# Two of eight channel groups of a depthwise convolution computed by GpSimd, as a product and an addition per tap

## The reference

```python
def conformer_conv(glu_in, pw1_b, dw_w, dw_b, ln_g, ln_b, w_o, b_o):
    a, gate = jnp.split(glu_in + pw1_b, 2, axis=-1)
    h = a * jax.nn.sigmoid(gate)
    h = causal_dwconv(h, dw_w) + dw_b
    h = jax.nn.silu(layernorm(h, ln_g, ln_b))
    return h @ w_o + b_o
...
        y_a = gated_deltanet(qkv, z, beta_logit, a_logit, ...)
        y_b = conformer_conv(glu_in, ...)
        g_a, g_b = jnp.split(jax.nn.sigmoid(gates), 2, axis=-1)
        y = (g_a * y_a + g_b * y_b) @ mix_w_out[i]
```

## Time and profile before

| | us |
|---|---|
| median of 3 runs | 3380.99 (3378.2 to 3381.55) |
| span of the profiled execution | 3380.1 |
| the page shows outside the span | nothing |
| TensorE, VectorE, ScalarE, GpSimd busy | 3065.2, 2050.7, 1397.9, 74.2 |

### The profile page before, as it was taken

How to read it: one execution, slowest core, us unless ns; L and a number is a source line. 1 busy time by engine, 2 the same in 40 slices (tenths; PEclk the granted TensorE clock), 3 DMA queues, 4 the chain that set the end, 5 groups by cost and what they waited for, 6 DMA issues and landing times.

```text
span 3380.1 us, 48537 instructions
## 1 busy us (share of the span) xinstructions
PE 3065.2 (91%) x18678; PEld 2694.5 (80%) x18678; DVE 2050.7 (61%) x3081; ACT 1397.9 (41%) x2230; POOL 74.2 (2%) x98
## 2 busy tenths in 40 slices
PE   8999888899999998888998889976999999987998
PEld 8989766789898986677997568864897989774897
DVE  5559887555555798856555455552656665553555
ACT  4446422343433552333434334442444345442444
POOL 0000000000000000000000000000000000000000
PEclk9999999899999999988998779986999999886999
DMA  6555211255455441114553235540554555421453
GB/s 215 186 163 170 86 50 51 99 166 187 164 181 175 163 156 38 57 49 158 186 187 119 71 109 187 181 141 6 184 187 163 175 182 184 162 94 50 153 187 137
DMA packets 127386, 469.89 MB, mean 139 GB/s; under 512 B 14318, under 2 KB 14494, under 8 KB 125904
## 3 DMA queue, kind: packets, MB, share of 16 engines
q1 hardware_dynamic: 124128, 452.62, 40.0%
q0 software_dynamic: 3056, 14.39, 1.2%
HBM read 465.91 MB, written 1.05 MB: 138 GB/s over the span
## 4 chain that ended last, share of the span: by engine, by line
PE 82%; DVE 10%; ACT 4%; issue 2%; POOL 1%; DMA 0%; SPq 0%; DVEq 0%; ACTq 0%
PE ps L469 81%; DVE hc L1623 1%; DVE w_lo_part L1422 1%; ACT w_hi_part L1034 1%; PE ps L537 1%; ACT gdn_w L1248 1%; POOL stats L2044 1%; DVE x_res L1546 1%; ACT h_hi_part L1050 0%; DVE x_res L1558 0%; DVE xn L1552 0%; DVE x_res L1525 0%; DVE h_lo_part L1438 0%; DVE lke L1865 0%; DMA w_raw<-in_weights 0%
## 5 line engine op out<-in xcount | busy, mean ns | idle before, releaser
L1422 DVE TENSOR_TENSOR w_lo_part<-w_raw,w_hi_part 128x1024 fp32r<-128x1024 f32 x856 | 1028.8, 1218 | 684.7 <-ACT w_hi_part L1034 684.2
L1034 ACT ACTIVATE w_hi_part<-w_raw 128x1024 fp32r<-128x1024 f32 x856 | 884.4, 1055 | 621.2 <-PE ps L469 615.5
L469 PE MATMUL ps<-h_hi_part,w_hi_part 128*128 128x256 f32 x3424 | 987.1, 288 | 16.5 <-DVE h_lo_part L1440 11.6
L469 PE MATMUL ps<-h_lo_part,w_hi_part 128*128 128x256 f32 x3424 | 983.3, 287 | 0.0
L469 PE MATMUL ps<-h_hi_part,w_lo_part 128*128 128x256 f32 x3424 | 982.7, 287 | 0.0
L469 PEld LDWEIGHTS ps<-h_hi_part,w_hi_part 128*128 128x128 f32 x3424 | 673.3, 197 | 24.3 <-issue 17.4
L469 PEld LDWEIGHTS ps<-h_lo_part,w_hi_part 128*128 128x128 f32 x3424 | 672.9, 197 | 0.6
L469 PEld LDWEIGHTS ps<-h_hi_part,w_lo_part 128*128 128x128 f32 x3424 | 672.2, 196 | 0.0
L469 PE MATMUL ps<-w_hi_part,h_hi_part 128*128 128x512 f32 (+2 forms) x812 | 329.8, 406 | 12.3 <-DVE h_lo_part L1438 7.0
L469 PE MATMUL ps<-w_hi_part,hid_lo_part 128*128 128x512 f32 x864 | 340.9, 395 | 0.0
L469 PE MATMUL ps<-w_lo_part,hid_hi_part 128*128 128x512 f32 x864 | 340.9, 395 | 0.0
(11 more groups left out here) (307 smaller groups left out, 2590.2 us busy)
## 6 DMA issues: line engine op xcount, KB each, us to landing
w_raw<-in_weights SPq DMA_DIRECT2D x856, 512.0 KB, 3.4
row<-in_rows POOLq DMA_DIRECT2D x8, 1024.0 KB, 4.9
row<-in_rows POOLq DMA_DIRECT2D x8, 512.0 KB, 4.4
const<-in_const SPq DMA_DIRECT2D x1, 1152.0 KB, 13.8
x_res<-in_x SPq DMA_DIRECT2D x1, 1024.0 KB, 5.3
ple_p<-in_p POOLq DMA_DIRECT2D x4, 256.0 KB, 4.9
out<-x_res SPq DMA_DIRECT2D x2, 512.0 KB, 2.6
cols<-in_cols SPq DMA_DIRECT2D x1, 422.0 KB, 7.1
```

The costliest lines, as they stand in the source:

```text
L469: return nc.tensor.matmul(out, lhsT, rhs_, start=start, stop=stop, skip_group_check=True)
L1034: A(w_hi[:, s, 0:wd], w_raw[:, s, 0:wd], ACT.Copy).then_inc(*up("w_hi", u))
L1422: V.tensor_tensor(w_lo[:, s, 0:wd], w_raw[:, s, 0:wd], w_hi[:, s, 0:wd].bitcast(F32), ALU.subtract).then_inc(*up("w_lo", u))
```

## The change

Of each four channel groups the fourth (3 and 7) is taken out of VectorE's rows and given to GpSimd, whose `conv_taps` runs through the same 31 taps with two instructions each: a product into a new tile `tap`, and an addition into `hc`. Each instruction waits for the one before. The rows stay where they are on VectorE, with three instructions instead of four. On GpSimd 16 taps stand behind the opening root of each of the four groups of `delta`, ahead of that group's closing root: 16, 16, 16 and the last 14 of 62. `conv_mean` on TensorE waits for the two channel groups by GpSimd's semaphore, and L1643 on VectorE gets a wait for the last of them.

```diff
+        tap = sb("conv_tap", [P, SEQ], F32, m1)
...
-                            pe.wait_ge(*when("conv", (tag, c)))
+                            pe.wait_ge(*when("conv_pool" if c % 4 == 3 else "conv", (tag, c)))
...
                     for k in range(CONVB):
-                        for c in range(first, first + 4):
+                        for c in range(first, first + 3):
...
                 dve.wait_ge(*when("ln_spread", (tag, 0)))
+                dve.wait_ge(*when("conv_pool", (tag, KC - 1)))
...
+            def conv_taps(tag, i):
+                for c in (KC // 2 - 1, KC - 1):
+                    pool.wait_ge(*when("glu", (tag, c)))
+                    for k in range(CONVB):
+                        w = col(("dww", i), c * CONVB + k)
+                        if k == 0:
+                            ins = nc.gpsimd.tensor_scalar(hc[:, c, :], glu[:, c, 0:SEQ], w, col(("dwb", i), c), ALU.mult, ALU.add)
+                        else:
+                            pool.wait_ge(*when("conv_pool", ("tap", tag, c, k - 1)))
+                            nc.gpsimd.tensor_scalar(tap[:, :], glu[:, c, k:k + SEQ], w, None, ALU.mult).then_inc(*up("tap", (tag, c, k)))
+                            pool.wait_ge(*when("tap", (tag, c, k)))
+                            ins = nc.gpsimd.tensor_tensor(hc[:, c, :], hc[:, c, :], tap[:, :], ALU.add)
+                        ins.then_inc(*up("conv_pool", ("tap", tag, c, k), *([(tag, c)] if k == CONVB - 1 else [])))
+                        yield
+
             def delta(tag, i):
+                taps = conv_taps(tag, i)
                 for t, g in ((t, g) for t in range(NT) for g in range(GROUPS)):
                     root(("g", (tag, t, g)), 8, gate[:, 10, 16:24])
+                    for _ in range(16):
+                        next(taps, None)
```

## The result

The changed kernel takes 3395.31 us (median of 5 runs, 3394.61 to 3397.52) against 3381.55 for the kernel before in the same session (3378.2 to 3382.96). The ratio is 1.0043, with a 95% interval of 1.003 to 1.0055: 14.5 us slower, where 27 were forecast.

A forecast was written before the change was run, and what follows sets the result against it. TensorE was taken as the bound (91% busy, 82% of the chain), VectorE's taps counting only within the chain. Eight groups losing 4.2 us make 34, less 7.3 credit is +27: 3381 + 27 = 3408 us, range 3371 to 3485.

The forecast's parts named there:

- company costs more than the tap row gives: In the delta-rule groups, GpSimd beside VectorE loses 34 us; VectorE's shorter tap rows give 7.3.
- The credit: VectorE's shorter tap rows save time only in the chain: 3.7 us a mixer, 7.3 us for two.
- the chain's ten rows: VectorE tap rows in a mixer's chain: seven save 0.395 us each, three beside GpSimd's closing root 0.3.
- The price of a GpSimd instruction: GpSimd's taps: 0.80 us an instruction, 0.88 with its wait, 1.76 a tap; VectorE loses 0.40 with two SBUF operands.
- 1.08 us an instruction: GpSimd's issue interval beside VectorE in a group's front: 0.40 + 0.48 + 0.20 us.
- the front: A delta group's start, VectorE L1723 to L1744, mostly two SBUF operands, all counted as chain: loses 3.7 us.
- the product at 0.7 and the addition at 0.9: Expected signs in the profile after: GpSimd's product lasts about 0.7 us, its addition about 0.9.
- the reading part of 0.40: Part of each GpSimd instruction, 0.40 us, during which VectorE waits if it wants two SBUF operands.
- the levels: Doubling levels of the triangular inverse, period 3.85 us: slack absorbs most delay, some 0.5 us a group lost.
- company costs nothing: Rival: VectorE keeps its turn and GpSimd fits in behind it; 3374 us, up to 3381; chance 0.33.
- GpSimd holds VectorE off for its whole instruction: Rival: VectorE is delayed the whole 0.80 us per GpSimd instruction; +118 us, 3499; chance 0.12.
- GpSimd as the bound: Rival: a GpSimd tap above 3.3 us makes closing roots and TensorE's mean late; at 4.0, 3456 us; chance 0.13.

The follow-up runs named there:

- e1_less_only: Against the change: GpSimd computes only the first tap of its two channel groups, the other 30 left out; 3379.09 us, ratio 0.9989.
- e2_company: Against the change: VectorE computes all eight channel groups again, GpSimd runs its 244 instructions beside it on an unused tile; 3414.64 us, ratio 1.0092.
- e7_memsets: VectorE computing all eight channel groups; against GpSimd's products and additions on an unused tile, 240 memsets in their place; 3382.47 us, ratio 1.0004.
- e9_one_group_late: Against the change: GpSimd has channel group 7 only, eight taps to a delta group, started behind the fourth doubling level; 3388.93 us, ratio 1.0018.

## Why the prediction was right, and where it was off

**Sign and mechanism.** The step that decided, that company costs more than the tap row gives, held: 18 us against 3.7. My sum had 34 against 7.3, so both terms were about twice too large and the net, 27, came out at 14.5. That they were too large by nearly the same factor is luck.

**The credit.** The three groups that have nine of the chain's ten rows saved 3.4 and 3.5 us where my sum has 3.3, but not in equal parts, and with other clocks. What I left out is the TensorE clock: the fourth group gave 1.4 us back in each mixer. I had read the clock of the stretches in the earlier trace rows (0.84 in the fourth) and made nothing of it.

**The price of a GpSimd instruction.** I took 0.80 us for both kinds, with 0.40 in which VectorE waits. Measured: an addition 0.72 to 0.74 when alone, a product 0.92 (0.48 in the other form); a tap 2.2 us on the mean where I had 1.76, 35 us for 16 in a group where I had 28 (the 1.08 us an instruction that I had for the front makes 2.16, which held). Of the signs, the product at 0.7 and the addition at 0.9 came out the other way round. Where an addition meets a two-operand VectorE instruction it costs VectorE 0.53 us at 512 columns and 0.40 a tap, so for that kind 0.40 was right or a little low; over all 120 additions it is 38 / 120 = 0.32. For the product it was far too high: 120 products cost 6 us in all, 0.05 each. The mean of the two kinds in the change, 18 us over 244 instructions, is 0.07 us; in my sum it was 34 / 244 = 0.14. The term that was mis-sized is thus the reading part of 0.40 for every GpSimd instruction: both kinds were given one price, and VectorE's loss was counted as if GpSimd won its turn each time. In the change the products mostly gave way.

**Front and levels.** I put 3.7 us of a group's 4.2 into the front and 0.5 into the levels. The change lost 1.8, 2.2, 1.4 and 2.0 us in the four fronts of the first mixer and 1.8, 0.8, 0.9 and 2.0 in those of the second (the taps' own relief taken in), and putting the start behind the front won some 11 us back in two mixers. The levels of the third group kept their period at first (3.85, 3.89, 3.99 us from L1768 to L1768), those of the first and fourth took up to 4.13. Against e1_less_only, which has the same rows of three and no company, the eight fronts are 14.6 us longer and the periods of the levels 4.6: together 19 us, about the 18 of company. So the place was right, the size of the front (1.8 us on the mean) half of what I said, and that of the levels, 0.6 a group, near my 0.5. The third group of the first mixer lost 3.6 us and that of the second 0.1 under the same instructions; TensorE ran at 0.87 and 0.95 of its clock there. Why the clock fell in one and not in the other stays open.

**The rivals.** That company costs nothing fell by e2_company; it holds within the interval for instructions that only write (e7_memsets). That GpSimd holds VectorE off for its whole instruction fell too: at most 0.53 us of the addition's 0.73, and far less beside products. The section Who interferes with whom of the Trainium skill's page SBUF — State Buffer has the right kinds (a VectorE instruction with two SBUF inputs and a GpSimd one that reads; a write does not count): the traces agree, L1765 kept 0.68 us and beside memsets all did. That the one which starts first holds the other off for its whole instruction, as that section has it for a shared pair of ports ("it's an exclusive lock"), they do not show: L1423 began 0.44 us behind the product and kept its 1.22. For the additions' length the page GPSIMD Engine Reference, Performance versus the Vector engine, was a good guide: it measures 4497 ns for 2048 columns, by an estimate 0.56 us for 256, beside 0.73 measured here with the fixed part. GpSimd as the bound fell by its 17 us and more of idle time before the closing roots.

## What to carry to other kernels

An elementwise loop handed to GpSimd was paid twice here: the credit is only the part of VectorE's time that stands in the chain, and each GpSimd addition, which reads two SBUF operands, can delay a two-operand VectorE instruction beside it. So look at what VectorE does in the stretch where GpSimd will run. In a stretch where VectorE is in the chain with SBUF operands the loan cost more than it gave; where VectorE waits for TensorE, or reads PSUM, it was nearly free, though no placement made the kernel faster. And a faster instruction on the side engine can make the kernel slower, if it brings the contact forward into the part that counts. Before a few us between two kernels are put down to an edit, the granted clocks have to be compared.

## What the runs showed of the hardware that I had not expected

- GpSimd's product of 256 columns takes 0.92 us in the one-operation form and 0.48 with a second operation, though that one does more.
- The product gives way to VectorE for long: 2.36 us in the change beside two VectorE instructions of full speed, 3.03 us once in e9_one_group_late. The addition doesn't: if it begins first, VectorE loses 0.40 to 0.53 us.
- 240 memsets of 0.31 us on GpSimd left VectorE's instructions as long as they were (taps 478 ns).
- TensorE's clock fell to 1.2 GHz ahead of the fourth group's state products in e1_less_only and in their midst in the kernel before, by the rows 2 us of the mixer. Executions of one and the same kernel at a mean clock of 0.922 and of 0.925 are 6 us or more apart. What moves the fall stays open.
